# Gate and up products of the feed-forward stages in three block groups, seven products in place of eight

## What is computed

```
def swiglu(x, w_in, w_out):
    gu = x @ w_in                  # (256, 1024) @ (1024, 2 * 2816)
    g, u = jnp.split(gu, 2, axis=-1)
    return (jax.nn.silu(g) * u) @ w_out
...
x = x + 0.5 * swiglu(rms_norm(x, ffn1_norm[l]), ffn1_w_in[l], ffn1_w_out[l])
```

## Time and profile before

| | |
|---|---|
| median of 3 runs | 1617.18 us (1617.08 to 1617.29) |
| profiled execution, first to last instruction | 1615.2 us |
| median less that span | 2.0 us |
| PE busy | 1606.5 us, 99% |
| DVE busy | 940.6 us, 58% |
| ACT busy | 789.6 us, 49% |

### The profile page before, as it was taken

How to read it: one execution, slowest core, us unless ns; L and a number is a source line. 1 busy time by engine, 2 the same in 40 slices (tenths; PEclk the granted TensorE clock), 3 DMA queues, 4 the chain that set the end, 5 groups by cost and what they waited for, 6 DMA issues and landing times.

```text
span 1615.2 us, 20528 instructions
## 1 busy us (share of the span) xinstructions
PE 1606.5 (99%) x7562; PEld 1335.9 (83%) x7562; DVE 940.6 (58%) x948; ACT 789.6 (49%) x941; POOL 161.3 (10%) x235
## 2 busy tenths in 40 slices
PE   9999999999999999999999999999999999999998
PEld 7888888888888888888888888888888888888887
DVE  6454656765545645465676554577754556874545
ACT  6444455554444544345555444466543446653444
POOL 1111112011000001111101000031100002110000
PEclk9999999999999999999999999999999999999999
DMA  9767655456655566756555665651665564366562
GB/s 283 254 202 227 214 194 163 164 184 217 203 186 176 189 218 212 228 201 196 170 165 174 232 209 182 201 181 67 215 219 189 173 202 162 105 216 196 167 201 91
DMA packets 209459, 308.02 MB, mean 191 GB/s; under 512 B 12452, under 2 KB 151096, under 8 KB 209400
## 3 DMA queue, kind: packets, MB, share of 16 engines
q1 hardware_dynamic: 205928, 300.66, 56.7%
q0 software_dynamic: 3168, 6.06, 1.4%
q10 hardware_dynamic: 304, 0.50, 0.1%
HBM read 304.00 MB, written 2.88 MB: 190 GB/s over the span
## 4 chain that ended last, share of the span: by engine, by line
PE 99%; ACT 0%; DVE 0%; issue 0%; POOLq 0%; POOL 0%; DVEq 0%; ACTq 0%
PE pg L1924 21%; PE pg L1926 21%; PE pg L1925 21%; PE acc L1924 10%; PE acc L1926 10%; PE acc L1925 10%; PE pg L2043 2%; PE pg L1937 1%; PE acc L2149 0%; PE acc L2131 0%; PE acc L2320 0%; PE acc L2278 0%; PE pg L2320 0%; PE acc L2289 0%; PE acc L2137 0%; PE acc L2116 0%
## 5 line engine op out<-in xcount | busy, mean ns | idle before, releaser
L1336 DVE TENSOR_TENSOR wlo<-raw,whi 128x2048 fp32r<-128x2048 f32 (+1 forms) x267 | 611.6, 2291 | 452.5 <-ACT whi L919 452.2
L919 ACT ACTIVATE whi<-raw 128x2048 fp32r<-128x2048 f32 (+1 forms) x267 | 509.5, 1909 | 318.7 <-PE acc L1926 153.3
L1924 PE MATMUL pg<-whi,xTh 128*128 128x512 f32 (+1 forms) x1456 | 575.4, 395 | 0.3 <-DVE wlo L1364 0.3
L1926 PE MATMUL pg<-whi,xTl 128*128 128x512 f32 (+1 forms) x1456 | 566.4, 389 | 0.0
L1925 PE MATMUL pg<-wlo,xTh 128*128 128x512 f32 (+1 forms) x1456 | 565.7, 389 | 0.0
L1924 PEld LDWEIGHTS pg<-whi,xTh 128*128 128x128 f32 x1456 | 273.4, 188 | 57.8 <-issue 1.7
L1926 PEld LDWEIGHTS pg<-whi,xTl 128*128 128x128 f32 x1456 | 273.2, 188 | 56.5
L1925 PEld LDWEIGHTS pg<-wlo,xTh 128*128 128x128 f32 x1456 | 273.6, 188 | 54.6 <-issue 1.0
L1924 PE MATMUL acc<-whi,bTh 128*128 128x512 f32 (+1 forms) x572 | 228.4, 399 | 0.0
L1926 PE MATMUL acc<-whi,bTl 128*128 128x512 f32 (+1 forms) x572 | 222.8, 390 | 0.0
L1925 PE MATMUL acc<-wlo,bTh 128*128 128x512 f32 (+1 forms) x572 | 221.8, 388 | 0.0
(11 more groups left out here) (241 smaller groups left out, 1064.9 us busy)
## 6 DMA issues: line engine op xcount, KB each, us to landing
raw<-in_ffn_w_in SPq DMA_DIRECT2D x172, 512.0 KB, 4.8
raw<-in_ffn_w_out SPq DMA_DIRECT2D x88, 512.0 KB, 4.2
raw<-in_w_gate_up SPq DMA_DIRECT2D x88, 512.0 KB, 4.6
raw<-in_mix_w_in SPq DMA_DIRECT2D x64, 512.0 KB, 4.3
raw<-in_w_down SPq DMA_DIRECT2D x44, 512.0 KB, 4.2
raw<-in_w_in SPq DMA_DIRECT2D x24, 512.0 KB, 4.6
raw<-in_mix_w_o SPq DMA_DIRECT2D x16, 512.0 KB, 4.3
raw<-in_w_o SPq DMA_DIRECT2D x16, 512.0 KB, 4.4
```

The costliest lines, as they stand in the source:

```text
L919: act_e.activation(whi[:, slot, 0:cols], raw[:, slot, 0:cols], ACT.Copy).then_inc(s.w_hi_ready, 1)
L1336: v.tensor_tensor(wlo[:, slot, 0:cols], raw[:, slot, 0:cols], f32(whi[:, slot, 0:cols]), ALU.subtract)\
L1924: pe.matmul(dst, xh, wh, start=first and i == 0, stop=False)
L1926: mm = pe.matmul(dst, xl, wh, start=False, stop=last and i == len(pairs) - 1)
```

## The change

The 11 steps of a stage become three groups and five plain steps. A group i joins steps 2+3i and 3+3i (512 gate and 512 up columns), with Strassen's scheme over 2x2 blocks: token tile by half of the rows, half of the rows by gate or up. It has seven products of 128x512 by 512x512 in place of eight; each takes one unit, 12 matmuls. Four of the seven weight operands are sums of blocks, which DVE makes as 128x2048 adds (`first_sum`, `second_sum`, `third_sum`, `fourth_sum`) in an area that the mixers use at other times; the up blocks are loaded there too (`up_k0`, `up_k1`), with their own semaphores. The four sums of activation blocks (`form`) are made once a stage from `joined_operand`, high part plus low part. The products are put together by six 128x512 operations of DVE (`combine_z` and the others), one copy by ACT (`first_product`), and two accumulations onto a bank (`onto`).

A stage now has 42 units (before 33): 27 loaded into `raw`, 3 up blocks and 12 sums split from where they lie. Plain steps run with the row half outermost. The order of a group on PE: product 0, plain step (first half), product 1, plain step (second half), product 2, product 3, down, product 4, down, product 5, down, product 6. The loops are written out. The gate biases of the mixer are loaded at the mixer's start instead of during the stage before it. Some semaphores are merged.

```diff
+GROUPS = 3
+SUM_UNITS = ((4, 6, 8, 9, 11, 13, 15), (16, 18, 20, 21, 23, 25, 27), (28, 30, 32, 33, 35, 37, 38))
+PLAIN_UNITS = ((0, 1), (2, 3), (5, 7), (17, 19), (29, 31))
+PLAIN_COLS = (0, 1, 4, 7, 10)
+DOWN_UNITS = (10, 12, 14, 22, 24, 26, 34, 36, 39, 40, 41)
+DOWN_ROWS = (0, 1, 4, 2, 3, 7, 5, 6, 10, 8, 9)
+FFN_UNITS = 42
...
+        up_k0, up_k1, w_sum, t2, t4 = (area(at, UNIT) for at in (4096, 6144, 8192, 10240, 2048))
+        x_full = xn[:, :, :].rearrange("p t d -> p (t d)").rearrange("p (k t n) -> p k t n", k=KC, t=TT)
+        form_at = (x_full[:, 4:8, 1], x_full[:, 0:4, 1], x_full[:, 0:4, 0], x_full[:, 4:8, 0])
+        form_h = [bTh[:, 4:6, :], bTh[:, 6:8, :]] + [form_parts[:, 0, :], form_parts[:, 1, :]]
+        form_l = [bTl[:, 4:6, :], bTl[:, 6:8, :]] + [form_parts[:, 2, :], form_parts[:, 3, :]]
...
+                plain(1, 0)
+                plain(1, 1)
+                for i in range(GROUPS):
+                    if i:
+                        sp.wait_ge(s.w_sum_ready, SUMS * (GROUPS * f + i - 1) + T3_AT)
+                    up_block(i, 0, up_k0)
+                    gate_block(i, 0)
+                    if i:
+                        sp.wait_ge(s.w_lo_ready, unit(0, rnd) + SUM_UNITS[i - 1][5] + 4)
+                    up_block(i, 1, up_k1)
+                    plain(2 + i, 0)
+                    plain(2 + i, 1)
+                    gate_block(i, 1)
+                    for d in range(3 * i, 3 * i + 3):
+                        if d != 2 + 3 * i or i < GROUPS - 1:
+                            down(d)
+                for d in range(8, STEPS):
+                    down(d)
...
+                def first_sum(i):
+                    v.wait_ge(chunk_landed[0], 16 + 32 * (GROUPS * f + i + 1))
+                    v.tensor_tensor(w_sum, gate_landed(i, 0), up_k0, ALU.add).then_inc(s.w_sum_ready, 1)
+
+                def second_sum(i):
+                    v.wait_ge(chunk_landed[1], 16 + 32 * (GROUPS * f + i + 1))
+                    v.wait_ge(s.w_sum_ready, sums_before(i) + T1_AT)
+                    v.tensor_tensor(t2, w_sum, up_k1, ALU.add).then_inc(s.w_sum_ready, 1)
+
+                def fourth_sum(i):
+                    v.wait_ge(s.w_sum_ready, sums_before(i) + T2_AT)
+                    v.tensor_tensor(t4, t2, gate_landed(i, 1), ALU.add).then_inc(s.w_sum_ready, 1)
+
+                def third_sum(i):
+                    v.tensor_tensor(w_sum, up_k0, up_k1, ALU.add).then_inc(s.w_sum_ready, 1)
...
+                def combine_z(i):
+                    v.wait_ge(s.p1_sb, GROUPS * f + i + 1)
+                    after(i, 1)
+                    if i == 0:
+                        v.wait_ge(s.form_lo, FORMS * (f + 1))
+                    else:
+                        v.wait_ge(s.act_ready, ACTS * f + 4 + 4 * i - 1)
+                    v.tensor_tensor(zw, pg[0][1][:, :], p1[:, :], ALU.subtract).then_inc(s.combined, 1)
+
+                def combine_u(i):
+                    after(i, 3)
+                    v.tensor_tensor(p1[:, :], pg[0][1][:, :], p1[:, :], ALU.add).then_inc(s.combined, 1)
...
+                def joined_operand():
+                    if start:
+                        v.wait_ge(s.first_lo, 2 * KC)
+                    else:
+                        v.wait_ge(s.xT_lo_ready, 4 * o + 4)
+                    v.tensor_tensor(xn[:, :, :].rearrange("p t d -> p (t d)"), f32(xTh[:, :, :]).rearrange("p k n -> p (k n)"),
+                                    f32(xTl[:, :, :]).rearrange("p k n -> p (k n)"), ALU.add).then_inc(s.form_sum, 1)
+
+                def form(m):
+                    a11, a12, a21, a22 = x_full[:, 0:4, 0], x_full[:, 4:8, 0], x_full[:, 0:4, 1], x_full[:, 4:8, 1]
+                    dst, one, other, op, at = ((a22, a21, a22, ALU.subtract, 1), (a21, a11, a21, ALU.subtract, 1),
+                                               (a11, a22, a11, ALU.subtract, 2), (a12, a11, a12, ALU.add, 4))[m]
+                    v.wait_ge(s.form_sum, (FORMS + 1) * f + at)
+                    v.tensor_tensor(dst, one, other, op).then_inc(s.form_sum, 1)
...
+                joined_operand()
+                form(0)
+                form(1)
+                form(2)
+                form(3)
                 if not start:
-                    refill(0, rnd + 1)
-                product(0, 0, 0)
-                product(1, 0, 0)
-
-                def product_lo(j, par):
-                    v.wait_ge(s.actT_hi, STEPS * f + j + 1)
-                    part = slice(2 * par, 2 * par + 2)
-                    v.tensor_tensor(bTl[:, part, :], pg[par][0][:, :].rearrange("p (c n) -> p c n", c=2),
-                                    f32(bTh[:, part, :]), ALU.subtract).then_inc(s.actT_lo, 1)
-
-                with v.Fori(0, (STEPS - 1) // 2) as jj:
-                    for par in range(2):
-                        j = 2 * jj + par
-                        product_lo(j, par)
-                        refill(1, rnd + j + 1)
-                        product(0, 1 - par, j + 1)
-                        refill(2, rnd + j + 1)
-                        product(1, 1 - par, j + 1)
-                        refill(0, rnd + j + 2)
-                product_lo(STEPS - 1, 0)
+                    loaded_lo(3)
+                form_lo_part(0)
+                product(0, 0)
+                product(0, 1)
+                form_lo_part(1)
+                first_sum(0)
+                for i in range(GROUPS):
+                    qa, qb = PLAIN_UNITS[2 + i]
+                    loaded_lo(SUM_UNITS[i][0])
+                    if i == 0:
+                        product_lo(0)
+                    loaded_lo(qa)
+                    if i == 0:
+                        product(1, 0)
+                        product(1, 1)
+                        second_sum(0)
+                    else:
+                        combine_gate1(i - 1)
+                        pair_product(i - 1, 0)
+                    summed_lo(i, 1)
+                    if i == 0:
+                        product_lo(1)
+                    loaded_lo(qb)
+                    fourth_sum(i)
+                    if i == 0:
+                        form_lo_part(2)
+                        form_lo_part(3)
+                    else:
+                        pair_product(i - 1, 1)
+                    loaded_lo(SUM_UNITS[i][2])
+                    combine_z(i)
+                    if i == 0:
+                        summed_lo(i, 3)
+                        third_sum(i)
+                        product(2 + i, 0)
+                    else:
+                        third_sum(i)
+                        product(2 + i, 0)
+                        summed_lo(i, 3)
+                    loaded_lo(DOWN_UNITS[3 * i])
+                    if i:
+                        product_lo(3 * i)
+                    product(2 + i, 1)
+                    combine_u(i)
+                    summed_lo(i, 4)
+                    if i:
+                        product_lo(3 * i + 1)
+                    combine_w(i)
+                    loaded_lo(DOWN_UNITS[3 * i + 1])
+                    summed_lo(i, 5)
+                    combine_up1(i)
+                    if i < GROUPS - 1:
+                        loaded_lo(DOWN_UNITS[3 * i + 2])
+                        product_lo(3 * i + 2)
+                        first_sum(i + 1)
+                        second_sum(i + 1)
+                        combine_up0(i)
+                        summed_lo(i, 6)
+                    else:
+                        summed_lo(i, 6)
+                        product_lo(3 * i + 2)
+                loaded_lo(DOWN_UNITS[8])
+                combine_up0(GROUPS - 1)
+                combine_gate1(GROUPS - 1)
+                pair_product(GROUPS - 1, 0)
+                pair_product(GROUPS - 1, 1)
+                loaded_lo(DOWN_UNITS[9])
+                product_lo(9)
+                loaded_lo(DOWN_UNITS[10])
+                product_lo(10)
+                if next_gain:
+                    refill(0, rnd + FFN_ROUNDS)
...
+                def summed(i, m, bank, operand, onto=False):
+                    u = SUM_UNITS[i][m]
+                    split_ready(u % SLOTS, rnd + u // SLOTS)
+                    product(bank[:, :], [(*operand(k), *weights(u % SLOTS, k * BANK, BANK)) for k in range(4)], first=not onto, onto=onto)\
+                        .then_inc(s.unit_done, 1)
...
-                step(0, 0, {(0, 1): lambda: turn(0, 0)}, first=True)
-                with pe.Fori(0, (STEPS - 3) // 2) as jj:
-                    step(2 * jj + 1, 1)
-                    step(2 * jj + 2, 0)
-                step(STEPS - 2, 1)
-                last_down(2, rnd + STEPS - 1)
+                plain(1, 0, 0)
+                plain(1, 1, 0).then_inc(s.unit_done, 1)
+                turn(b_y, act, 0, 2)
+                plain(1, 0, 1).then_inc(s.ffn_t0_done, 1)
+                plain(1, 1, 1).then_inc(s.unit_done, 1)
+                for i in range(GROUPS):
+                    if i:
+                        combined(i - 1, UP0_AT)
```

(58 more changed lines are left out.)

379 lines of the change are left out of this document (262 added, 117 removed).

## The result

| | before | after |
|---|---|---|
| median | 1617.2 us (4 runs) | 1591.71 us (4 runs, 1591.2 to 1592.52) |
| ratio to before, 95% interval | | 0.9843 [0.9829, 0.9857] |
| span of the profiled run | 1615.2 us | 1590.3 us |

The kernel is 1.6% faster. The forecast was 1586 with a range of 1575 to 1605; the time lies in the range, 5.7 us above the forecast and 0.7 us above the forecast's own range of 1580 to 1591.

What follows compares the result with a forecast made beforehand. PE was taken as the bound nearly everywhere: span 1615.2 - 49.0 (matmuls) + 12.5 (five later stage starts) + 5.4 (first stage) = 1584.1 us, plus 2.0 around it, gives 1586 us; range 1575 to 1605.

Steps and rivals of the forecast that it cites:

- Matmuls: On PE in the feed-forward stages: 216 matmuls fewer at 0.2267 us each, 49.0 us saved.
- DVE in a group: DVE's work in a full group: 42.9 us of PE's 47.6 us, so it fits with 10% spare.
- the row of the same shape: The float32 128x2048 sums were priced at 2.21 us, like a split; 2.5 us was the upper bound.
- Groups 1 and 2: The later two groups of each stage: every DVE result ready before PE asks, no stall in 12 groups.
- the closest place: combine_w before product 4 in a group: ready 0.5 us before PE asks.
- Stage starts: PE waits for silu products, then a low part: 2.5 us in each of five stages, 5.4 us in the first.
- Transfers: Up blocks for second_sum land in 4.3 us, in time, costing nothing; upper bound 5 us over 12 handovers.
- the two reserves of 0.5 and 1.6 us: Spare time for a late up block: 0.5 us before second_sum, 1.6 us at product 6's low part behind it.
- no clock loss: The forecast sum held no clock term: the earlier trace showed no fall of PE's clock after 2 us idle.
- the fourth rival: PE's clock drops to 1.2 GHz after the first stage's 3.8 us stop, for as long again: 1590 us, chance 0.05.
- at a pitch of 0.227: The pitch of PE's matmuls, read from the old kernel's timeline as 0.2267 us, was expected in the profile after.

Runs made afterwards that it cites:

- the experiment ahead of combine_w: Changed kernel plus one unused 128x2048 DVE sum right before combine_w in groups 1 and 2 of each stage, 12 in all: 1612.38 us, ratio 0.997.
- the kernel with the idle products: Changed kernel plus 14 matmuls with unused results ahead of the first turn of the first stage, where PE stood waiting: 1589.89 us, ratio 0.9832.
- the last two kernels: Changed kernel with all helpful edits and combine_w right behind combine_u in group 0: 1579.55 us; the same with form_parts and work allocated first: 1577.29 us.

## Why the prediction was nearly right

**Matmuls.** 216 went, at 0.2267 each: 49.0 us. The mixer behind the first stage hides neither a gain nor a loss: between the rows of `x` shown above lie 148.88 us before and 148.89 after.

**DVE in a group.** 43.4 for 42.9 us, the sums 2.28 us, priced by the split as the row of the same shape. The pitch of 2.21 holds for them too: in the rows of the experiment ahead of combine_w the sum at 447.61 is followed at 449.80, 2.19 us later.

**Groups 1 and 2.** No stop, as laid out. The added sum measured the closest place: 0.58 us of slack for 0.5 in the forecast.

**Stage starts.** 0.75 + 1.50 = 2.25 us for 2.5, in each of five stages; first stage 3.67 + 1.50 = 5.2 for 5.4. Place and cause were right, shown by removing the turn's and the down's stop each alone.

**Transfers.** The landing was 5.0 us, not 4.3, and it still cost nothing; the two reserves of 0.5 and 1.6 us covered it.

**What was mis-sized.** The step "no clock loss" failed: the fourth rival, given a chance of 0.05, happened inside the forecast's own stop, for 1.6 us and not 4. The fall lasted until about 33 us, some 3 us: the turn and the matmul behind it took 0.36 us longer than in the kernel with the idle products, and six matmuls lost 0.2 us each. The rule of the Trainium skill, "TensorE: Matmul & The Clock Gate", section "What's actually happening", that an idle TensorE falls back to half clock and earns the full one by sustained work, is borne out by the stops of 3.7 us and, in the kernel with the silu products first, 2.8 us from start to start; behind the stops of 1.5 us in the other stages the granted clock stayed at 1.00.

The step "at a pitch of 0.227" failed for 432 of the matmuls that stayed: on `form_parts` it was 0.234, 3.0 us. The forecast took the pitch of the old operands for that of a new one.

With 0.6 us for the late unit in this execution (20.15 for 19.54) and 1.5 us less of stops than forecast, 1584.1 + 1.6 + 3.0 + 0.6 - 1.5 = 1587.8; 2.5 us of the span stay open. They lie in the feed-forward stages, where the mean pitch of the other matmuls, from the first turn of a stage to its last, went from 0.2270 to 0.2275 us; over the 4104 of them that would be some 1.8 us. Whether DVE's and ACT's added traffic does that was not tried. In the first stage the terms add up to almost the whole gain of 8.2 us: 5.2 of stops, 1.6 of clock, 0.6 for the late unit, 0.5 on `form_parts`.

That the forecast came within 5.7 us is in part luck: the stops, laid out 1.5 us too long, hid some of what was left out.

## What to carry to other kernels

When an engine with spare time takes over work in a fixed order, lay its list against the bound engine's requests operation by operation: the same 2.2 us cost nothing or 1.6 us each, depending on its place. An idle wait on another engine's result is where a small operation with ready inputs belongs, and a wait inherited from a step that used to stand there must be asked for again by the step that now does. A stall of the matmul engine can cost more than its length, and filling it with useless matmuls gave that part back.

## What the runs showed of the hardware

The same 128x512 matmul has a pitch of 0.227 or 0.234 us, 3% apart at a granted clock of 1.00, with the stationary operand in the same tensor; how the buffers are laid out in memory decides which, and not the address of that operand alone.

A 128x2048 operation of DVE that starts while POOL is at one of 512 columns or more is stretched, and POOL's is stretched when it starts second. In the fourth stage of the changed kernel POOL folds two gains, and the low part beside it takes 4.07 us where 2.29 is usual; timelines of POOL, then DVE:

```profile
906.49 2.40 POOL L875 TENSOR_TENSOR gain_a<-gain_a,gain_m 128x1024 f32<-128x1024 f32 x1 [38.76 <-DMA gain_a<-in_attn_norm]
```

```profile
906.98 4.07 DVE L1592 TENSOR_TENSOR wlo<-work,whi 128x2048 fp32r<-128x2048 f32 x1
```

POOL ends at 906.49 + 2.40 = 908.89, and the low part at 911.05, 2.16 us later: nearly a whole operation's time after POOL's end. In the first stage both orders follow each other: POOL starts while one DVE operation is running, and the next DVE operation starts while POOL is. Timelines of DVE, then POOL:

```profile
149.94 2.29 DVE L1592 TENSOR_TENSOR wlo<-work,whi 128x2048 fp32r<-128x2048 f32 x1
152.37 3.16 DVE L1592 TENSOR_TENSOR wlo<-raw,whi 128x2048 fp32r<-128x2048 f32 x1
```

```profile
150.50 2.88 POOL L845 TENSOR_TENSOR shared<-shared,consts_a 128x512 f32<-128x512 f32 x1 [15.19 <-PE pg L2241]
```

The first DVE operation keeps its 2.29 us. POOL takes 2.88 us, where the same operation takes 1.29 at 156.36, beside small DVE operations only. The second DVE operation ends at 155.53, 2.15 us after POOL's end at 153.38. All seven such operations of the changed kernel end 2.15 or 2.16 us after POOL's end, and both of the kernel before. The Trainium skill, "SBUF — State Buffer", section "Who interferes with whom", says that the two engines share a port pair under an exclusive lock, and that a DVE instruction with two inputs in SBUF contends with a POOL instruction that reads SBUF; these rows agree. In the fourth stage it cost nothing, but in the kernel with third_sum later the same operation (2.89 us) was on the path, and the combine_w stop of that stage was 1.3 us and not 0.7. In the last two kernels it is the longest stop before product 4, 1.2 and 0.8 us. No run took POOL's operation away.
